# Moving a 128x4 square root three places later in ScalarE's queue, in a two-block decoder on one core

## The reference

```python
def step(state, inp):
    r_t, w_t, k_t, v_t, a_t, b_t = inp
    sa = jnp.einsum('bhij,bhj->bhi', state, a_t)
    state = (state * w_t[:, :, None, :] + sa[..., None] * b_t[:, :, None, :]
             + v_t[..., None] * k_t[:, :, None, :])
    y_t = jnp.einsum('bhij,bhj->bhi', state, r_t)
    return state, y_t
...
y = jnp.moveaxis(ys, 0, 1)
mean = jnp.mean(y, axis=-1, keepdims=True)
var = jnp.mean(jnp.square(y - mean), axis=-1, keepdims=True)
yn = ((y - mean) * lax.rsqrt(var + RWKV_GN_EPS)).reshape(B, S, D)
yn = yn * gn_g.astype(jnp.float32) + gn_b.astype(jnp.float32)
bonus = jnp.sum(rh * kh * r_k.astype(jnp.float32), axis=-1, keepdims=True) * vh
out = (yn + bonus.reshape(B, S, D)).astype(x.dtype)
return (out * g) @ w_o
```

## Time and profile before

| what | value |
|---|---|
| median of three runs | 3876.8 us (3872.47 to 3878.14) |
| profiled execution | 3872.47 us, span 3870.7 us |
| TensorE busy | 3686.3 us, 95% of the span |
| VectorE, ScalarE, GpSimd busy | 44%, 39%, 33% |
| turns 1 to 15 of the RWKV loop | 3089 to 3280 us of the span, 15 turns |
| one turn in the middle of it | 13.30 us |

### The profile page before, as it was taken

One profiled execution on the slowest core, in us unless ns is written; L12 is line 12 of the kernel. 1 busy time (PEld: TensorE's weight loads), 2 busy tenths in 40 slices (PEclk: granted clock), 3 DMA queues, 4 the chain that ended last, 5 costly groups with the idle time before them and its releaser, 6 DMA issues.

```text
span 3870.7 us, 47558 instructions
## 1 busy us (share of the span) xinstructions
PE 3686.3 (95%) x17456; PEld 2904.1 (75%) x17456; DVE 1698.9 (44%) x2436; ACT 1497.0 (39%) x2440; POOL 1271.2 (33%) x584
## 2 busy tenths in 40 slices
PE   8989998999899999989998999999999999999997
PEld 7777786888687777868886677788844588777886
DVE  2443447542424433574434743604247544526042
ACT  3246633432322566233324644423225143444232
POOL 4421133444343112334443143344300011433443
PEclk9989999999999899999999999999999999999999
DMA  3221111323223111222232322222322200322222
GB/s 135 99 70 44 44 66 66 104 97 103 86 93 109 41 43 49 71 87 97 94 106 89 104 93 71 82 98 95 107 87 70 78 2 1 107 73 83 96 95 81
DMA packets 100352, 310.92 MB, mean 80 GB/s; under 512 B 25952, under 2 KB 26080, under 8 KB 99552
## 3 DMA queue, kind: packets, MB, share of 16 engines
q1 hardware_dynamic: 81792, 298.90, 22.9%
q10 hardware_dynamic: 18400, 9.78, 0.9%
HBM read 302.35 MB, written 5.24 MB: 79 GB/s over the span
## 4 chain that ended last, share of the span: by engine, by line
issue 45%; PE 38%; POOL 15%; ACT 1%; DMA 0%; DVE 0%; POOLq 0%; DVEq 0%; ACTq 0%; SPq 0%
POOL ring_r L2667 15%; PE ps L447 9%; PE ps L449 9%; PE ps L448 9%; PE ps L953 2%; PE ps L1053 1%; PE ps L791 1%; PE ps L617 1%; PE ps L972 1%; PE ps L1129 0%; PE ps L1098 0%; PE ps L1111 0%; PE ps L1089 0%; PE ps L1131 0%; PE ps L1121 0%
## 5 line engine op out<-in xcount | busy, mean ns | idle before, releaser
L2667 POOL TENSOR_TENSOR ring_r<-ring,rounded_r 128x1024 fp32r<-128x1024 f32 x504 | 1233.5, 2450 | 2120.7 <-ACT rounded_r L1234 2120.4
L447 PE MATMUL ps<-source_hi,rounded_r 128*128 128x512 f32 x2560 | 1020.5, 399 | 93.9 <-DVE X_lo L1950 31.3
L1234 ACT ACTIVATE rounded_r<-ring 128x1024 fp32r<-128x1024 f32 x504 | 533.5, 1059 | 1331.6 <-PE ps L449 1190.9
L448 PE MATMUL ps<-source_hi,ring_r 128*128 128x512 f32 x2560 | 1008.0, 394 | 0.0
L447 PEld LDWEIGHTS ps<-source_hi,rounded_r 128*128 128x128 f32 x2560 | 487.5, 190 | 212.6 <-DVE X_lo L1950 33.7
L449 PE MATMUL ps<-X_lo,rounded_r 128*128 128x512 f32 x1536 | 603.1, 393 | 0.0
L448 PEld LDWEIGHTS ps<-source_hi,ring_r 128*128 128x128 f32 x2560 | 487.9, 191 | 101.8 <-issue 2.6
L449 PEld LDWEIGHTS ps<-X_lo,rounded_r 128*128 128x128 f32 x1536 | 291.5, 190 | 62.1
L449 PE MATMUL ps<-N_lo,rounded_r 128*128 128x512 f32 x768 | 303.2, 395 | 0.0
L2210 DVE SCALAR_TENSOR_TENSOR T<-ps,PAR,T 128x511 f32<-128x511 f32 (+1 forms) x176 | 131.5, 749 | 229.3 <-ACT T L1427 214.4
L447 PE MATMUL ps<-H_hi,rounded_r 128*128 128x512 f32 x512 | 199.2, 389 | 0.0
(11 more groups left out here) (501 smaller groups left out, 5654.2 us busy)
## 6 DMA issues: line engine op xcount, KB each, us to landing
ring<-in_weights SPq DMA_DIRECT2D x560, 512.0 KB, 3.3
X<-in_x SPq DMA_DIRECT2D x2, 1024.0 KB, 7.0
out_x<-X SPq DMA_DIRECT2D x4, 512.0 KB, 2.6
SWAP<-Z ACTq DMA_DIRECT2D x4, 256.0 KB, 3.3
MEM<-in_mem ACTq DMA_DIRECT2D x1, 1024.0 KB, 4.7
mem_keys<-Z ACTq DMA_DIRECT2D x1, 1024.0 KB, 3.9
diag_in<-Y ACTq DMA_DIRECT2D x8, 128.0 KB, 2.2
Z<-diag_in ACTq DMA_DIRECT2D x8, 128.0 KB
```

The lines of the kernel that those rows point to most:

```text
L447: mm(o, lh, rh, start=start, stop=False)
L448: mm(o, ll, rh, start=False, stop=False)
L1234: av(RH[:, j, :], ring[:, j, :], ACT.Copy).then_inc(w_hi, 1)
L2667: nc.gpsimd.tensor_tensor(RL[:, j, :], ring[:, j, :], RH[:, j, :].bitcast(F32), ALU.subtract).then_inc(w_lo, 1)
```

## The change

`output_root(u - 1)` is called two steps later in each turn u >= 1 of ScalarE's loop: no longer ahead of `right_copied` of the lower half, but behind it and behind `below_copied(u + 1)`.

```diff
                     x0_turned(u + 1)
                 else:
                     round_chunk(B_RWO // RING, 1)
-                if u >= 1:
-                    output_root(u - 1)
                 right_copied(u, lower, "pb", "pbc")
                 if after:
                     below_copied(u + 1)
+                if u >= 1:
+                    output_root(u - 1)
                 solution_copied(u, lower, "ub", "ubc")
                 if after:
                     inverse_copied(u + 1)
```

## The result

The changed kernel took 3912.7 us (median of 4 runs, 3907.2 to 3915.3), the kernel before 3877.5 us beside it (3872.5 to 3878.8): a ratio of 1.009 with a 95% interval of [1.0079, 1.0102]. It is 35.2 us slower. The forecast was 18 us slower, and a range up to 3903 us; the time lies outside it.

A forecast was written before the change was run, and what follows sets the result against it. TensorE, busy for the whole turn, was taken as the bound. 13 turns at 1.33 us, 1.1 us for turn 14 and 0 for turn 15 gave 18.4 us, on the median 3876.8 a forecast of 3895 us, range 3885 to 3903.

The forecast's parts named there:

- TensorE bounds the stage: TensorE is busy for all 13.30 us of a turn, so a later start of L1178 finds no idle time.
- step 4: TensorE starts L1178 0.05 us after L2585 ends, near 3138.86 instead of 3137.53: 1.33 us later in a turn.
- the forecast sum: Turns 1 to 13 at 1.33 us, 17.3 us; turn 14, 1.1 us; turn 15, 0: 18.4 us.
- Steps 1 and 2: On ScalarE the root starts at 3137.59 behind L1826's second copy, without overlap; VectorE's reciprocal follows 0.03 us after its end.
- Step 3: VectorE's L2585 arrives 0.08 us into GpSimd's third operation, is held until 3138.38 and ends at 3138.80; 0.42 us when alone.
- The rival in which it slips in ahead: VectorE's multiplication L2585 runs before GpSimd's operation: 1.00 to 1.11 us a turn, 14.0 to 15.6 us in all; 32%.
- The other side: Rival: on ScalarE the root held the copy L1837, so it comes 0.29 us sooner each turn; 4.4 us faster, 3872; 4%.
- Against a lower clock: Argument that TensorE's clock stays at 1.00, since the new turns would be busy for 13.30 of 14.6 us.
- under 9%: Rival: both GpSimd operations go first, or TensorE's clock falls from the new gaps; 27 us at the contention end, 3904.
- So I take 0: Turn 15: L2585 starts just as GpSimd's subtraction ends, L1178 comes within 0.1 us of its old place; price 0.
- The other end: Turn 15: GpSimd's next subtraction, 2.35 us, gets in first; L1178 is 2.3 us late, less the product's gap: +1.9 us.

The follow-up runs named there:

- experiment 5: Changed kernel with GpSimd's blocks (L2701) for units u >= 3 also waiting for yn of unit u-3; 3906.7 against 3877.8 us for the kernel before.
- experiment 1: Kernel before with the root moved behind the copy L1837 only, still ahead of L1826, in all turns; 3883.4 against 3878.9 us.
- experiment 2: Kernel before with the change in turn 15 alone, 3883.1 against 3878.9 us; and with it in all turns but 15, 3908.2 us.
- experiment 3: Changed kernel with five extra 128x128 matmuls on TensorE in each turn before its wait for yn; 3900.0 against 3878.9 us for the kernel before.

## Why the prediction was wrong

- **TensorE bounds the stage; a wait there is paid in full.** Right. A turn that keeps its clock is 1.33 us longer, the figure of step 4, and turns 1 to 14 without the clock's part make 18.4 us, the forecast sum.
- **Steps 1 and 2, the root behind L1826 without overlap, the reciprocal 0.03 us later.** Right: root 3146.79 behind 3146.76, reciprocal at 3147.12.
- **Step 3, GpSimd holds L2585.** Right: 0.62 us for 0.42, where 0.64 was worked out, and 0.42 when GpSimd is moved away (experiment 5). The rival in which it slips in ahead fell.
- **The other side, that the root held L1837.** Fell: the copy kept its idle time (1.05 us, where it had 0.87), and experiment 1, which only takes the root from before it, gained nothing.
- **"Against a lower clock: the last turn is busy for 11.40 of 12.60 us and keeps 1.00."** This step failed, and with it the sum put the slow clock at nothing. It is a third of the measured price in turns 1 to 14 alone, 11.4 us, and 14.7 us with turn 15's part. I took the busy share of a stretch as the measure, and the last turn's 1.2 us of idle time are two pieces, of 0.47 and 0.73 us. One such turn is also too few: behind gaps of 0.76 us the clock fell in only 4 cases of 14. The new kernel has one gap in each of 14 turns, 1.27 us in 13 of them and 1.07 us in turn 14, and 7 were followed by 3.4 us at 1.2 GHz. The mechanism stood in the list of rivals, under 9%, with a price only for contention.
- **"So I take 0" for turn 15.** Failed too: 5.2 us in the profile, 4.1 us by experiment 2. The other end was named, GpSimd's next subtraction first: 2.3 us less the product's gap, +1.9 us. That is what the wait costs by experiment 3, where the clock stays up. What was missing even there is the slow clock behind that wait, 3.3 us in the changed kernel. With L2585 due at 3277.35 and GpSimd's next operation at 3277.40, I chose the side that costs nothing without a row that spoke for it. The arrival was also mis-timed. I let L1837 begin where the root had begun, at 3276.39, which is 1.34 us behind the start of GpSimd's first subtraction; it began 1.46 us behind it (3308.30 and 3306.84), and L2585 came 0.15 us after the second subtraction had started.
- **What the sum lacked.** The 18.4 us of waiting in turns 1 to 14 came out to the decimal, and each step of it was seen in the trace. Without the 14.7 us of slow clock the change would have cost some 20 us by the profile, inside the range.

## What to carry to other kernels

On an engine that is full and at its full clock, a new wait costs its length and then, in some of the cases, the slow stretch behind it: price both, by the length of the single gap and the number of times it comes, not by the busy share. Before a small step is moved later in a queue, look at what the instruction now ahead of it waits for; one copy further back cost nothing in turns 1 to 14, two more cost 1.33 us a turn. Where such a wait can't be avoided, put ready work of the same engine in front of it: that took away two thirds of the price, and even useless matmuls were better than idling.

## What the runs showed of the hardware that was not expected

- Behind a single gap in a turn that is otherwise full, TensorE's clock fell to 1.2 GHz for 3.41 us: in none of 13 cases at 0.27 us, in 4 of 14 at 0.76 to 0.77 us, in 6 of 14 at 1.07 us (experiment 5), in 7 of the 13 or 14 of each of three kernels at about 1.27 us, and in all 14 at 2.24 us. A fall cost 1.63 us; behind turn 15's longer wait the clock stayed low for 3.4, 6.8 or 10.2 us.
- GpSimd and VectorE hold each other up in both directions, and the one that comes first wins. L2585 took 0.62 us when GpSimd's small operation was first, 2.49 us when a 128x1024 one was (2.35 us by itself); in experiment 1 L2585 was first, and GpSimd's operation took 0.64 us instead of 0.45.
- Five more matmuls of 128x128 in each turn made the changed kernel 12.6 us faster.
